# Stick-breaking scores of two heads made together on 64 rows each, with filler evacuations moved between the heads' steps

## The reference

```python
z = jnp.einsum('bhqd,bhkd->bhqk', qb, k) * scale          # scale = 1/8
strict = key_idx[None, :] < q_idx[:, None]
log_one_minus = jnp.where(strict, jax.nn.log_sigmoid(-z), 0.0)
suffix = lax.cumsum(log_one_minus, axis=3, reverse=True) - log_one_minus
w = jnp.where(strict, jnp.exp(jax.nn.log_sigmoid(z) + suffix), 0.0)
out = jnp.einsum('bhqk,bhkd->bhqd', w, v)
```

## Time and profile before

| what | value |
|---|---|
| median of 3 runs | 1368.15 us (1366.32 to 1369.08) |
| profiled execution | 1365.55 us, span 1363.7 us |
| mean granted TensorE clock | 0.976 |
| TensorE matmul | busy 1261.9 us, 93% |
| VectorE | busy 703.6 us, 52% |
| ScalarE | busy 499.2 us, 37% |
| GpSimd | busy 102.3 us, 7% |
| chain that ended last | TensorE 74%, VectorE 13%, ScalarE 8% |

### The profile page before, as it was taken

The page is one execution under the profiler, slowest core; times in us unless marked ns, Lnnn a source line. Parts: engine busy times, 40 slices in busy tenths (PEclk is TensorE's granted clock), DMA queues, the critical chain, the costliest instruction groups (busy, mean ns, idle before and its releaser), DMA issues.

```text
span 1363.7 us, 14956 instructions
## 1 busy us (share of the span) xinstructions
PE 1261.9 (93%) x6048; PEld 1006.0 (74%) x6048; DVE 703.6 (52%) x1070; ACT 499.2 (37%) x793; POOL 102.3 (7%) x81
## 2 busy tenths in 40 slices
PE   2799899999998998999999899898999999999985
PEld 0578767776775776777776799686888888888864
DVE  3852575458456566537665675445433333333346
ACT  3462343444444343425446412223322322322233
POOL 7310111013000000000000300100000000000001
PEclk8799899999999998999999999999999999999998
DMA  7722232112120333221112000022323223333212
GB/s 287 278 78 77 89 123 92 63 50 94 46 78 32 108 120 110 73 97 47 62 47 78 16 1 1 5 73 77 108 97 104 93 93 95 130 102 109 94 51 85
DMA packets 35221, 118.16 MB, mean 87 GB/s; under 512 B 4000, under 2 KB 4256, under 8 KB 35152
## 3 DMA queue, kind: packets, MB, share of 16 engines
q1 hardware_dynamic: 33824, 112.68, 24.9%
q0 software_dynamic: 1328, 4.52, 1.1%
HBM read 112.99 MB, written 4.19 MB: 86 GB/s over the span
## 4 chain that ended last, share of the span: by engine, by line
PE 74%; DVE 13%; ACT 8%; issue 3%; POOL 1%; DMA 1%; DVEq 0%; SPq 0%; ACTq 0%
PE pb L608 72%; DVE wlo L1676 2%; ACT whi L1203 1%; DVE xT L1676 1%; ACT mP L1392 1%; PE pb L863 1%; DVE gq L1679 1%; DVE mnm L1899 1%; ACT fP L1392 1%; PE pb L706 1%; DMA xT<-x_d 1%; DVE fP L1895 1%; PE pb L690 1%; DVE tmpf L1679 1%; DVE mP L1910 1%
## 5 line engine op out<-in xcount | busy, mean ns | idle before, releaser
L608 PE MATMUL pb<-hhi,wlo 128*128 128x512 f32 x1048 | 413.9, 395 | 16.7 <-ACT hhi L1203 9.0
L608 PE MATMUL pb<-hhi,whi 128*128 128x512 f32 x1048 | 412.2, 393 | 0.0
L608 PE MATMUL pb<-hlo,whi 128*128 128x512 f32 x1048 | 399.4, 398 | 12.7 <-DVE wlo L1676 4.4
L1676 DVE TENSOR_TENSOR wlo<-raw,whi 128x1024 fp32r<-128x1024 f32 (+1 forms) x178 | 223.2, 1262 | 218.0 <-ACT whi L1203 217.4
L608 PEld LDWEIGHTS pb<-hhi,wlo 128*128 128x128 f32 x1048 | 198.7, 190 | 64.8 <-ACT hhi L1203 12.7
L608 PEld LDWEIGHTS pb<-hlo,whi 128*128 128x128 f32 x1048 | 198.5, 189 | 61.3 <-DVE wlo L1676 12.0
L608 PEld LDWEIGHTS pb<-hhi,whi 128*128 128x128 f32 x1048 | 198.8, 190 | 42.1
L1203 ACT ACTIVATE whi<-raw 128x1024 fp32r<-128x1024 f32 (+1 forms) x178 | 181.2, 1034 | 81.1 <-PE pb L608 81.0
L608 PE MATMUL pb<-ahi,whi 128*128 128x512 f32 x176 | 68.5, 389 | 0.0
L608 PE MATMUL pb<-ahi,wlo 128*128 128x512 f32 x176 | 68.5, 389 | 0.0
L608 PE MATMUL pb<-alo,whi 128*128 128x512 f32 x176 | 68.5, 389 | 0.0
(11 more groups left out here) (319 smaller groups left out, 1722.8 us busy)
## 6 DMA issues: line engine op xcount, KB each, us to landing
raw<-w_all SPq DMA_DIRECT2D x173, 512.0 KB, 3.5
adab<-ada_d SPq DMA_DIRECT2D x16, 512.0 KB, 9.3
raw<-w_all SPq DMA_DIRECT2D x10, 384.0 KB, 3.1
xT<-x_d SPq DMA_DIRECT2D x8, 256.0 KB, 8.5
ple_scratch<-zs SPq DMA_DIRECT2D x8, 256.0 KB, 2.6
xT<-x_d POOLq DMA_DIRECT2D x8, 256.0 KB, 3.0
out_d<-xT SPq DMA_DIRECT2D x8, 256.0 KB, 2.3
plr<-ple_scratch POOLq DMA_DIRECT2D x4, 256.0 KB, 3.5
```

The source lines that it names most:

```text
L608: return e.matmul(out, lhs, rhs, start=start, stop=stop, skip_group_check=True)
L1676: return e.tensor_tensor(out, a, b, op)
```

## The change

The query tile has one slot per two heads: both halves of the rows hold data, ScalarE copies a whole bank at once (4 copies, not 8), and GpSimd's clearing with its semaphore goes. `sb_qk` takes a pair: for each key block a matmul on rows 0 to 63 and one on rows 64 to 127, then the masks of one head, then of the other. On TensorE the scores of a pair come together, after the values of the pair before; the order in a pair is filler, suffix, filler, suffix, filler, filler, values, scores of the next pair, filler. VectorE and ScalarE do `sb_pre` of both heads, then a filler step, and so on as below. On ScalarE the Silu block of the third pair stands ahead of the fourth pair's `sb_pre`; before it stood behind it. The number of fillers is the same.

```diff
--- before.py
+++ after.py
@@ -237,7 +237,7 @@
             rn = sb(pre, "rn", [128, S])
             rk = sb(pre, "rk", [128, S])
         with ExitStack() as s1:
-            qp = sb(s1, "qp", [128, 8, S])
+            qp = sb(s1, "qp", [128, 4, S])
             kp = sb(s1, "kp", [128, 4, S])
             sbv = sb(s1, "sbv", [128, 4, S])
             sp = sb(s1, "sp", [128, 2, 1280])
@@ -394,8 +394,7 @@
         MODS = sig("dve_mods", range(NB))
         ZPLE = sig("act_zple", range(8))
 
-        QZERO = sig("pool_qzero", (0, 1))
-        QPE, KPE, SBV = sig("act_qp", range(8)), sig("dve_kp", range(4)), sig("act_sbv", range(4))
+        QPE, KPE, SBV = sig("act_qp", range(4)), sig("dve_kp", range(4)), sig("act_sbv", range(4))
         SBQK, SBMIN, SBLN, SBMAX, SBHI, SBLO0, SBLO1, SBSUF = (
             sig(n, range(8)) for n in ("pe_sbqk", "dve_sbmin", "act_sbln", "dve_sbmax", "act_sbhi", "pool_sblo",
                                        "dve_sblo", "pe_sbsuf"))
@@ -513,7 +512,6 @@
                 e.tensor_tensor(dst, buf[64:96, 0, :], buf[64:96, 1, :], ALU.add).then_inc(ROPED.sem, 1)
 
             def sb_low(h):
-                G.wait_ge(*QZERO(1))
                 G.wait_ge(*SBHI(h))
                 if h > 1:
                     G.wait_ge(*ROPED("kr"))
@@ -549,13 +547,6 @@
             G.wait_ge(*GPS.tick())
             e.tensor_scalar(ang[:, :], ang[:, :], lim, -lim, ALU.min, ALU.max).then_inc(ANG.sem, 1)
 
-            G.wait_ge(*ROPE())
-            G.wait_ge(*proj("pp", 1, 3))
-            for r in range(2):
-                if r:
-                    G.wait_ge(*QZERO(0))
-                e.memset(qp[64 - 64 * r:128 - 64 * r, :, :].rearrange("p (m r) n -> p m r n", r=2)[:, :, r, :], 0.0
-                         ).then_inc(QZERO.sem, 1)
             for h in range(8):
                 sb_low(h)
                 if h == 1:
@@ -712,7 +703,7 @@
 
             project_group([("sbq", i, 128, i) for i in range(4)], h1)
             for m in range(4):
-                free[m] = [QPE(2 * m + 1)]
+                free[m] = [QPE(m)]
             for m in range(4):
                 project("sbk", m, 128, 4 + m, h1)
                 free[4 + m] = [KPE(m)]
@@ -749,17 +740,20 @@
                     free[b] = [GA67(m)]
                 yield
 
-            def sb_qk(h):
-                T.wait_ge(*QPE(h))
-                T.wait_ge(*QZERO(h % 2))
-                T.wait_ge(*KPE(h // 2))
+            def sb_qk(pr):
+
+                T.wait_ge(*QPE(pr))
+                T.wait_ge(*KPE(pr))
                 T.wait_ge(*CONST())
                 for kb in KB_ORDER:
-                    out = sb_out(h, kb)
-                    bank(3 * (h % 2) + BK[kb])
-                    mm(out, kp[:, h // 2, 128 * kb:128 * kb + 128], qp[:, h, 128 * kb:512], kb != 3, False)
-                    t = mm(out[:, 0:128], identB, msB, False, False)
-                t.then_inc(SBQK.sem, 1)
+                    for r in range(2):
+                        bank(3 * r + BK[kb])
+                        rows = slice(64 * r, 64 * r + 64)
+                        mm(sb_out(r, kb), kp[rows, pr, 128 * kb:128 * kb + 128], qp[rows, pr, 128 * kb:512], kb != 3, False)
+                for r in range(2):
+                    for kb in KB_ORDER:
+                        t = mm(sb_out(r, kb)[:, 0:128], identB, msB, False, False)
+                    t.then_inc(SBQK.sem, 1)
 
             def sb_suffix(h):
                 i = h % 2
@@ -796,17 +790,15 @@
             next(fa)
             for pr in range(4):
                 h = 2 * pr
-                sb_qk(h + 1)
                 next(fa)
                 sb_suffix(h)
                 next(fa)
-                if pr < 3:
-                    sb_qk(h + 2)
+                sb_suffix(h + 1)
                 next(fa)
-                sb_suffix(h + 1)
                 next(fa)
                 sb_pv(pr)
                 if pr < 3:
+                    sb_qk(pr + 1)
                     next(fa)
             next(fa)
 
@@ -1271,9 +1263,7 @@
             A.wait_ge(*TRIG("cos"))
             for m in range(4):
                 A.wait_ge(*proj("sbq", m))
-                for r in range(2):
-                    copy(qp[64 * r:64 * r + 64, 2 * m + r, :], PB[m][64 * r:64 * r + 64, :], scale=0.125
-                         ).then_inc(QPE.sem, 1)
+                copy(qp[:, m, :], PB[m][:, :], scale=0.125).then_inc(QPE.sem, 1)
             for m in range(4):
                 conv("sbk", m)
             for c in range(4):
@@ -1334,29 +1324,26 @@
                     e.activation(sp[:, h % 2, 512 * b:512 * b + n], PB[3 * (h % 2) + b][:, 0:n], ACT.Exp).then_inc(SBW.sem, 1)
 
             fa = filler_a()
-            sb_pre(0)
-            sb_pre2(0)
-            next(fa)
             for pr in range(4):
                 h = 2 * pr
+                sb_pre(h)
+                sb_pre(h + 1)
+                next(fa)
+                sb_pre2(h)
                 next(fa)
                 sb_weights(h)
-                sb_pre(h + 1)
-                next(fa)
                 sb_pre2(h + 1)
                 next(fa)
                 sb_weights(h + 1)
                 next(fa)
+                next(fa)
                 if pr < 3:
-                    sb_pre(h + 2)
-                    next(fa)
                     if pr == 2:
                         e.preload_act_table_set(SILU)
                         for m in range(8):
                             A.wait_ge(*ZE(m))
                             e.activation(zs[:, m, :], zs[:, m, :], ACT.Silu).then_inc(SIL.sem, 1)
                         e.preload_act_table_set(EXPLN)
-                    sb_pre2(h + 2)
             next(fa)
 
             A.wait_ge(*ZA(3))
@@ -1828,33 +1815,33 @@
                     v = sp[:, h % 2, 512 * b:512 * b + n]
                     t = tt(v, PB[3 * (h % 2) + b][:, 0:n], v, ALU.max)
                 t.then_inc(SBMAX.sem, 1)
+
+            def sb_low(h):
                 V.wait_ge(*SBHI(h))
                 if h:
                     V.wait_ge(*SBSUF(h - 1))
                 tt(spl[:, 1024:], sp[:, h % 2, 1024:], fr(sph[:, 1024:]), ALU.subtract).then_inc(SBLO1.sem, 1)
 
             fa = filler_a()
-            sb_pre(0)
-            sb_pre2(0)
-            next(fa)
             for pr in range(4):
                 h = 2 * pr
-                next(fa)
+                sb_pre(h)
                 sb_pre(h + 1)
                 next(fa)
+                sb_pre2(h)
                 sb_pre2(h + 1)
+                sb_low(h)
+                next(fa)
+                sb_low(h + 1)
+                next(fa)
                 next(fa)
                 next(fa)
                 V.wait_ge(*SBPV(pr))
-                e.tensor_copy(qp[:, h, :], PB[6][:, :]).then_inc(OA.sem, 1)
-                if pr < 3:
-                    sb_pre(h + 2)
-                    next(fa)
-                    sb_pre2(h + 2)
+                e.tensor_copy(qp[:, pr, :], PB[6][:, :]).then_inc(OA.sem, 1)
             for m in range(4):
                 V.wait_ge(*SIL(m))
                 V.wait_ge(*OA(m))
-                tt(zs[:, m, :], zs[:, m, :], qp[:, 2 * m, :], ALU.mult).then_inc(ZA.sem, 1)
+                tt(zs[:, m, :], zs[:, m, :], qp[:, m, :], ALU.mult).then_inc(ZA.sem, 1)
             next(fa)
 
             for k in range(5):
```

## The result

| | before | changed |
|---|---|---|
| median | 1367.46 us, 5 runs (1364.38 to 1369.08) | 1375.71 us, 5 runs (1373.11 to 1377.51) |
| ratio | | 1.0059, 95% interval 1.0041 to 1.0076 |
| profiled execution | 1365.55, span 1363.7 | 1373.37, span 1371.6 |

The changed kernel is slower by 8.25 us between the medians; 9.0 was forecast. The profiled executions differ by 7.8.

What follows compares the result with a forecast made beforehand. TensorE, busy 93% of the span, bounds the kernel by its own work and holes. New holes 21.6 + clock 3.4 - scores 8.3 - old holes 7.7 = +9.0 us: median 1377.2, range 1370 to 1386.

Steps and rivals of the forecast that it cites:

- Scores: TensorE's scores: row halves run side by side, 2.75 us a pair, 3.6 the first; a gain of 8.3 us.
- Old holes gone: TensorE's four old waits in the stage, 7.1 us, disappear; with record tails 7.7 us gained.
- The four holes: After each pair's scores, the filler's evacuation comes late behind both heads' work on VectorE and ScalarE: 4.3 us each, 17.2 lost.
- Smaller new holes: Adjacent fillers before the values lose 2 x 1.0 + 0.3 = 2.3 us; the latent norm after the second pair 2.1.
- The 2.1 after the second pair: Latent norm's work ahead of a filler's evacuation, plus one more set of maxima: 2.1 us lost, bounds 0 and 3.1.
- Clock: TensorE's clock drops after each new hole: net 0 at the first two pairs, 1.7 us each at third and fourth, 3.4.
- Sum: All terms: 21.6 + 3.4 - 8.3 - 7.7 = +9.0 us on the profiled execution, median 1377.2.
- A: Rival: row halves don't overlap on TensorE, a pair takes 5.0 us instead of 2.75; +8.5, 1385.7; chance 0.12.
- B: Rival: the four filler evacuations are not late, 17.2 and the clock's 3.4 go; -11.6, 1356.6; chance 0.06.
- C: Rival: later waits at 338.81 and 429.69 and 1.7 of clock absorb 7.7 us; +1.3, 1369.4; chance 0.07.
- D: Rival: second suffixes also come late, up to 1.9 us four times; +7.6, 1384.8; chance 0.05.

Runs made afterwards that it cites:

- scores in turn: Changed kernel with all of one head's score matmuls of a pair first, then all of the other's: 1381.92 us, ratio 1.0108.
- Rounding between: Changed kernel with ScalarE's rounding of a weight chunk put between the exp/ln of a pair's first head and the second's: 1361.25 us, ratio 0.9958.
- copy out first: Changed kernel with VectorE's copy out of the bank ahead of its subtraction, in fillers from the second gate on: 1369.07 us, ratio 1.0016.
- rounding between, with banks: Changed kernel with ScalarE's rounding between both heads' exp/ln, four fillers in bank 6, VectorE's first-suffix subtraction before the second head's maxima: 1356.79 us, ratio 0.9924.
- other bank: Changed kernel with the first filler after the third and fourth pairs' scores in bank 6 instead of 7: 1370.05 us, ratio 1.0017.

## Why the prediction was right

- **Scores.** 2.79 a pair for 2.75 and 3.54 for 3.6: a gain of 20.2 - 11.9 = 8.3, as forecast. The column halves of the values' product were the right row for row halves: 2.36 (223.96 - 221.60) beside 2.31. So the smaller gain that the Trainium skill's efficiency of 3.07 in four would give ("TensorE: Matmul & The Clock Gate", Part 3) did not come with two halves: 2.36 for a pair is what one head alone takes on its 64 rows in the scores in turn. That run also shows the price of another order, 1.6 a pair.
- **Old holes gone.** True of all four waits; the GpSimd waits did not come back. That the latent norm's wait stayed away was luck: the half clock hid it (below).
- **The four holes.** The waits are 4.10, 4.07, 4.11 and 4.11, and 4.3 is lost with the record's tail: as forecast, and nearly so at the rope filler (4.05 lost). Rounding between shows the second exp and ln as 2.55 of it; copy out first shows that the evacuation and not the weights was late.
- **Smaller new holes.** The two of 1.0 came (0.88 and tail), the 0.3 did not show. The 2.1 after the second pair did not come at all: TensorE ran its filler at half clock and reached that place late. Rounding between brings a wait of 1.77 there, so the queue was judged rightly; I had written that the one could hide behind the other, and so set the hole of 2.1 there and nothing for the clock. The runs had it the other way round, no hole and 2.6 of clock.
- **Clock.** It fell with all four waits. That is about 6 us net of before, where 3.4 and the 2.1 were set: 0.5 short.
- **Sum.** -8.3 - 7.7 + 17.1 + 2.1 + 6 = 9.2; the stage measured 8.8. Most of the last 0.4 is in the old waits: taken from start to start they cost 3.66 + 1.67 + 2.18 + 0.50 = 8.0, and not 7.7. That the medians differ by 8.25, so near to 9.0, says less than the stage does: the start 0.6 later and the regain of 1.6 were in no term.
- **Rivals.** A (halves don't overlap) did not happen. Its price of 8.5 was about right: with 5.15 a pair, as estimated above, it would be 3 x 2.36 + 1.6 = 8.7. The scores in turn cost 6.5, because 0.75 of each pair still overlaps. B (copies in time) did not happen, but is what the copy-out-first run makes of two pairs. C (later holes absorb): the waits after 338 us have nearly the same length, 2.69 and 3.30, but of its three terms the clock's 1.7 did go in the profiled execution (above); 7.7 was far too much. D (late second suffix): no such wait.

## What to carry to other kernels

Packing two small products side by side paid 8.3 us here, but it also took away the pieces of TensorE work that stood between projections sharing one bank, and doubled what stood ahead of a weight's rounding in another engine's queue. When steps are merged, list for each shared buffer what now lies between its writer and the next one, and put the step that frees or feeds the busiest engine ahead of the merged work in every queue; that order was worth 15 us of this stage. The four holes of over 4 us cost their length, 17.1 us, and about half as much again in clock.

## What the runs showed of the hardware

The order in which VectorE's and GpSimd's subtractions start decides how long VectorE's takes. Each has two inputs in SBUF. VectorE and GpSimd in order of time, changed kernel:

```profile
237.06 2.33 DVE L1663 TENSOR_TENSOR spl<-sp,sph 128x256 fp32r<-128x256 f32 x1
```

```profile
236.99 2.11 POOL L520 TENSOR_TENSOR spl<-sp,sph 128x896 fp32r<-128x896 f32 x1 [32.97 <-ACT sph L1195]
```

The same in the run "rounding between, with banks":

```profile
226.09 0.42 DVE L1664 TENSOR_TENSOR spl<-sp,sph 128x256 fp32r<-128x256 f32 x1 [1.34 <-ACT sph L1196]
226.44 1.61 DVE L1664 TENSOR_TENSOR sp<-pb,sp 128x512 f32<-128x512 f32 x3
```

```profile
226.14 2.34 POOL L520 TENSOR_TENSOR spl<-sp,sph 128x896 fp32r<-128x896 f32 x1 [31.13 <-ACT sph L1196]
```

In the first case VectorE's began 0.07 us after GpSimd's, took 2.33 and ended 0.29 after it; it looks as if VectorE got through only once GpSimd was done. In the second it began 0.05 ahead, took 0.42, and GpSimd's took 2.34 and not 2.11. VectorE's maxima, which have one input in PSUM, took 1.61 us beside GpSimd's, as they do in the same trace without it (223.14). That is why the suffix in several runs waited for VectorE's small share and not for GpSimd's large one, and why turning the two round gained little.

Whether TensorE's clock falls after a wait of 2.7 us is not fixed by its length. After the wait on `kc`, 2.69 in both kernels, it fell before and not after the change. The run "other bank" has both within one execution, behind its two suffix waits of 2.67:

```profile
239.00:243.00 4.00, 3.53 (x19) 3.20 (x20) 2.06 (x3) 1.38 (x4) 0.04 (x1) 1.00 0.33 114
282.00:286.00 4.00, 3.96 (x14) 3.72 (x15) 1.62 (x2) 0.27 (x1) 0.00 (x0) 0.57 0.36 131
```
